# Two transformer blocks in one kernel: depthwise-convolution sums kept in a PSUM bank as two column halves, activation sums split once and reloaded, angle tables moved up, a fifth query unit before the first turn

## The reference, cut to what matters

```python
h = rmsnorm(x) * (1 + scale) + shift          # scale, shift, gate = c @ w_ada + b_ada
glu_a, glu_b, z_conv, q, k, v, z_att, g_conv, g_att = split(h @ w_in)
u = glu_a * sigmoid(glu_b)
u = depthwise_conv(u, conv_w, 31 taps, causal) + conv_b
y_conv = (silu(layernorm(u)) * silu(z_conv)) @ w_conv_out
q, k = partial_rope(q), partial_rope(k)       # cos and sin of position * frequency
# three groups of 8 heads: causal windows with dilation 1, 4, 16; softmax over <= 256 keys
y_att = (merge(three groups) * silu(z_att)) @ w_att_out
x = x + gate * ((sigmoid(g_conv) * y_conv + sigmoid(g_att) * y_att) @ w_o)
```

## Time and the profile before

| | |
|---|---|
| median of 3 runs | 2749.54 us (2749.19 to 2750.30) |
| the profiled execution's own time | 2753.2 us |
| its span | 2751.4 us, granted clock 0.958 |
| PE busy | 2522.0 us (92%), 11800 matmuls |
| DVE busy | 1732.1 us (63%) |
| ACT, POOL busy | 924.9 us (34%), 911.3 us (33%) |
| transfers | 339.09 MB, mean 123 GB/s |

### The profile page before, as it was taken

The page is one execution under the profiler, slowest core; times in us unless marked ns, Lnnn a source line. Parts: engine busy times, 40 slices in busy tenths (PEclk is TensorE's granted clock), DMA queues, the critical chain, the costliest instruction groups (busy, mean ns, idle before and its releaser), DMA issues.

```text
span 2751.4 us, 31479 instructions
## 1 busy us (share of the span) xinstructions
PE 2522.0 (92%) x11800; PEld 2050.0 (75%) x11800; DVE 1732.1 (63%) x2561; ACT 924.9 (34%) x1745; POOL 911.3 (33%) x797
## 2 busy tenths in 40 slices
PE   7899999976779977789999999999999999999997
PEld 4687767954657955557788887887888778787886
DVE  7613668977678878855744653122438686858789
ACT  4114431132321133235500413233116635545453
POOL 3436653525544435642342423222421000000000
PEclk9999989988889988889999999999999999999998
DMA  7413231122332133254433402222527757685754
GB/s 281 129 50 134 96 122 36 62 89 81 102 127 65 55 117 108 94 184 149 146 107 123 150 25 87 74 70 75 182 96 227 201 152 200 153 213 115 208 133 112
DMA packets 180939, 339.09 MB, mean 123 GB/s; under 512 B 21682, under 2 KB 60850, under 8 KB 174260
## 3 DMA queue, kind: packets, MB, share of 16 engines
q1 hardware_dynamic: 160868, 288.33, 31.6%
q0 software_dynamic: 18768, 44.57, 9.0%
q10 hardware_dynamic: 1152, 4.19, 0.4%
HBM read 265.53 MB, written 63.12 MB: 119 GB/s over the span
## 4 chain that ended last, share of the span: by engine, by line
PE 64%; DVE 20%; ACT 5%; issue 4%; DMA 4%; POOL 3%; SPq 1%; DVEq 0%; ACTq 0%; POOLq 0%
PE ps L2737 35%; PE ps L2994 19%; DVE scr L2032 11%; PE ps L2884 4%; POOL w_lo L1323 2%; PE ps L2861 2%; ACT scr L1535 2%; PE ps L2766 1%; PE ps L2847 1%; DMA raw<-in_w_in 1%; ACT w_hi L1575 1%; PE ps L2837 1%; POOL w_hi L1321 1%; DVE w_lo L2096 1%; DVE w_lo L2473 1%
## 5 line engine op out<-in xcount | busy, mean ns | idle before, releaser
L2032 DVE SCALAR_TENSOR_TENSOR scr<-scr,small 128x512 f32<-128x512 f32 x480 | 496.9, 1035 | 15.6
L1321 POOL CAST w_hi<-raw 128x512 fp32r<-128x512 f32 x216 | 157.1, 727 | 801.9 <-DMA raw<-in_w_in 436.7
L2737 PE MATMUL ps<-w_hi,act_hi 128*128 128x512 f32 (+1 forms) x960 | 382.4, 398 | 14.1 <-POOL w_lo L1323 12.6
L2737 PE MATMUL ps<-w_hi,act_lo 128*128 128x512 f32 (+1 forms) x960 | 373.6, 389 | 0.0
L2737 PE MATMUL ps<-w_lo,act_hi 128*128 128x512 f32 (+1 forms) x960 | 373.0, 389 | 0.0
L2994 PE MATMUL ps<-w_hi 128*128 128x512 f32 x896 | 350.6, 391 | 11.0 <-issue 7.5
L2994 PE MATMUL ps<-w_lo,w_hi 128*128 128x512 f32 x896 | 349.4, 390 | 0.0
L2994 PE MATMUL ps<-w_hi,w_lo 128*128 128x512 f32 x896 | 349.2, 390 | 0.0
L2737 PE MATMUL ps<-act_hi,w_hi 128*128 128x512 f32 x768 | 306.8, 399 | 18.0 <-POOL w_lo L1323 6.8
L2737 PE MATMUL ps<-act_lo,w_hi 128*128 128x512 f32 x768 | 305.5, 398 | 0.0
L1323 POOL TENSOR_TENSOR w_lo<-raw,w_hi 128x512 fp32r<-128x512 f32 x216 | 299.2, 1385 | 17.3
(11 more groups left out here) (280 smaller groups left out, 4266.6 us busy)
## 6 DMA issues: line engine op xcount, KB each, us to landing
raw<-in_w_in SPq DMA_DIRECT2D x136, 256.0 KB, 3.2
w_lo<-form_d SPq DMA_DIRECT2D x21, 1024.0 KB, 5.6
late_hi<-h2c_d SPq DMA_DIRECT2D x21, 1024.0 KB, 7.6
raw_c<-in_w_in SPq DMA_DIRECT2D x27, 512.0 KB, 4.7
vreg<-in_w_ada SPq DMA_DIRECT2D x36, 256.0 KB, 5.4
raw<-in_w_in SPq DMA_DIRECT2D x18, 512.0 KB, 4.8
raw<-in_w_up POOLq DMA_DIRECT2D x8, 1024.0 KB, 11.6
late_lo<-in_w_up SPq DMA_DIRECT2D x8, 1024.0 KB, 5.5
```

The costliest lines, as they stand in the source:

```text
L1321: pool.tensor_copy(dhi, src).then_inc(w_hi_done, 1)
L2032: nc.vector.scalar_tensor_tensor(ca, u_in[:, j:j + HALF], w[:, j:j + 1], ca, ALU.mult, ALU.add).then_inc(tap, 1)
L2737: ins = nc.tensor.matmul(out_, lhs, rhs, start=(m == 0), stop=(m == 3 * nk - 1))
```

## The change

1. **Taps.** The running sum of a piece lives in PSUM bank 6 (`ps_c`), and every tap is two instructions on 256 columns. Half e of a tap waits for half e of the tap before, the last but one instruction. The last tap writes `ca` in SBUF, and it alone waits for the store of the piece before. The plan is now 2 a step from step 28 on in g = 0, then 4 a unit, 2 a step, 4 a unit, 2 a step. In a round, DVE's order is: masks and maxima, two steps' taps, evictions, one step's taps, evictions, one step's taps.
2. **Forms.** Only the first four reloads of g = 0 are split by ACT and DVE. Their two parts are stored to DRAM (`parts_d`), and so are the two parts of a21, straight from the projection stage. The other 23 reloads bring both parts, 1 MB each, with nothing for ACT or DVE to do. The store of the plain a21, and DVE's wait for it, go.
3. **Angle tables.** DVE computes the angles ahead of its first block of x, and the two argument reductions behind the second and fourth block; they lie in `ev_more`. SP issues the load of the positions ahead of the adaptive weights.
4. **Order in projection stage 0.** q4 comes before the turn of q0; qt1 and qt2 follow q5 and q6 and so on, and k0 comes before qt6. The loop that runs units together still has four.
5. Waits for the stores of the forms are split by form.

```diff
@@ plan
-                if (t, g) == ("q", 0) and B < LEAD:
+                if (t, g) == ("q", 0) or (t, g, B) == ("k", 0, 0):
                     late.append((t + "t", g, B))
-                    if B == LEAD - 1:
-                        us.append(late.pop(0))
+                    n = {("q", 4): 1, ("q", 5): 2, ("q", 6): 2, ("q", 7): 1, ("k", 0): 1}.get((t, B), 0)
+                    us += late[:n]
+                    late = late[n:]
@@ tap_plan
-    give([("step", 0, s) for s in range(26, 64)], 1)
-    give([(t, 1, B) for t in "qkv" for B in range(NB)], 5)
+    give([("step", 0, s) for s in range(28, 64)], 2)
+    give([(t, 1, B) for t in "qkv" for B in range(NB)], 4)
@@ build
+        ps_c = ps[6][:, :]
-        angs, angc, turns = (scr[:, i * 256:(i + 1) * 256] for i in range(3))
+        angs, angc, turns = (ev_more[:, i // 2, 256 * (i % 2):256 * (i % 2) + 256] for i in range(3))
@@ form_load (SP)
+                if fresh(g, i):
+                    sp.dma_start(form_part(place, 1).bitcast(F32),
+                                 form_d[FORM_DRAM[name]].rearrange("p (k n) -> p k n", k=4)).then_inc(form_ld[place], 16)
+                    return
+                for part in range(2):
+                    sp.dma_start(form_part(place, part).bitcast(F32),
+                                 parts_d[FORM_DRAM[name], part].rearrange("p (k n) -> p k n", k=4)
+                                 ).then_inc(form_ld[place], 16)
+            def parts_store(name, place):
+                for part in range(2):
+                    sp.dma_start(parts_d[FORM_DRAM[name], part].rearrange("p (k n) -> p k n", k=4),
+                                 form_part(place, part).bitcast(F32)).then_inc(parts_st[name], 16)
@@ block_io (SP)
+                if g == 0 and i in (3, 5, 7, 9):
+                    sp.wait_ge(form_lo, (i - 1) // 2)
+                    name = FORM_SEQ[(i - 3) // 2]
+                    parts_store(name, FORM_PLACE[name])
@@ qkv_io (SP)
+                    if u == ("k", 0, 7):
+                        sp.wait_ge(lo_done, SPLIT_LO[("h", 3)])
+                        parts_store("a21", A_SLOT)
@@ DVE, start
+            angles()
             for B in range(NB):
                 x_scale(B)
+                if B in (1, 3):
+                    angle_turns(*((0.0, angs), (0.25, angc))[B // 2])
...
-            dve.wait_ge(a21_st, A21_ST0 + 16)
@@ conv_taps (DVE)
+                    if j == TAPS - 1 and m:
+                        dve.wait_ge(c_st, 16 * m)
+                    for e in range(2):
+                        here, there = slice(256 * e, 256 * e + 256), slice(j + 256 * e, j + 256 * e + 256)
+                        if t:
+                            dve.wait_ge(tap, 2 * t + e - 1)
+                        if j == 0:
+                            nc.vector.tensor_scalar(ps_c[:, here], u_in[:, there], w[:, 0:1],
+                                                    c_cb[:, m // 2:m // 2 + 1], ALU.mult, ALU.add).then_inc(tap, 1)
+                        else:
+                            dst = ca if j == TAPS - 1 else ps_c
+                            nc.vector.scalar_tensor_tensor(dst[:, here], u_in[:, there], w[:, j:j + 1],
+                                                           ps_c[:, here], ALU.mult, ALU.add).then_inc(tap, 1)
@@ block_act_unit (ACT), block_unit_out (DVE)
-                if i in FORM_AT:
+                if i in FORM_AT and fresh(g, FORM_AT.index(i)):
@@ attention (DVE)
-                    for i in units_in(g, b, d):
+                    conv_taps(("step", g, 4 * r))
+                    conv_taps(("step", g, 4 * r + 1))
+                    for i in units_in(g, b, c):
                         block_unit_out(g, i)
-                    for n in range(4):
-                        conv_taps(("step", g, 4 * r + n))
+                    conv_taps(("step", g, 4 * r + 2))
+                    for i in units_in(g, c, d):
+                        block_unit_out(g, i)
+                    conv_taps(("step", g, 4 * r + 3))
```

More of the change, by code:

```diff
@@ L598, in form_part, with fresh, wait_form_load, wait_form @@
             return (w_hi, w_lo)[part][:, 0, k0:k0 + 4, :]
+        def fresh(g, i):
+            return g == 0 and i < FRESH
         def form_loads(g, i):
-            place = FORM_PLACE[FORM_SEQ[i]]
-            per = sum(1 for x in FORM_SEQ if FORM_PLACE[x] == place)
-            return g * per + sum(1 for x in FORM_SEQ[:i + 1] if FORM_PLACE[x] == place)
+            place, n = FORM_PLACE[FORM_SEQ[i]], 0
+            for g_ in range(g + 1):
+                for i_ in range(FORMS if g_ < g else i + 1):
+                    if FORM_PLACE[FORM_SEQ[i_]] == place:
+                        n += 1 if fresh(g_, i_) else 2
+            return n
+        def wait_form_load(eng, g, i):
+            place = FORM_PLACE[FORM_SEQ[i]]
+            eng.wait_ge(form_ld[place], FORM_LD0[place] + 16 * form_loads(g, i))
+        def wait_form(eng, g, i):
+            if fresh(g, i):
+                eng.wait_ge(form_lo, i + 1)
+            else:
+                wait_form_load(eng, g, i)
+        def wait_form_stored(eng, name):
+            eng.wait_ge(form_st[name], FORM_ST0[name] + 16)
+        def wait_parts_stored(eng, name):
+            eng.wait_ge(parts_st[name], PARTS_ST0[name] + 32)
         def block_act(p, part):
@@ L828, in form_load @@
                 place = FORM_PLACE[name]
-                if g == 0 and i == 0:
-                    sp.wait_ge(a21_st, A21_ST0 + 16)
-                    sp.wait_ge(form_st, FORM_ST0 + 16 * 4)
+                if fresh(g, i):
+                    wait_form_stored(sp, name)
+                if g == 0 and i >= 2:
+                    old = {2: "a21", 3: "s2", 4: "s4", 5: "s1", 8: "s3"}.get(i)
+                    if old:
+                        wait_parts_stored(sp, old)
                 if i < 3:
@@ L839, in form_load @@
                     wait_block(sp, 3 * g + 2, 7, 1)
-                sp.dma_start(form_part(place, 1).bitcast(F32),
-                             form_d[FORM_DRAM[name]].rearrange("p (k n) -> p k n", k=4)).then_inc(form_ld[place], 16)
+                if fresh(g, i):
+                    sp.dma_start(form_part(place, 1).bitcast(F32),
[9 more added lines that the diff above has]
+                                 form_part(place, part).bitcast(F32)).then_inc(parts_st[name], 16)
             def block_store(n, p, t):
@@ L935, in conv_load @@
                 if m >= 2:
-                    sp.wait_ge(tap, TAPS * (m - 1))
+                    sp.wait_ge(tap, 2 * TAPS * (m - 1))
                 for hh in range(h + 1):
@@ L946, in conv_store @@
                 t, h = m // 2, m % 2
-                sp.wait_ge(tap, TAPS * (m + 1))
+                sp.wait_ge(tap, 2 * TAPS * (m + 1))
                 sp.dma_start(feature_tile(c_d, t, h), ca).then_inc(c_st, 16)
@@ L1380, in _ @@
                     wait_block(pool, c - 2, 4, 1)
+                if c == 3 and s == 0:
+                    wait_parts_stored(pool, "s1")
                 split_piece(n, raw[:, n % RAW, :], w_hi[:, buffer_of(c), s, :], w_lo[:, buffer_of(c), s, :])
@@ L1488, in qkv_unit @@
                 elif name in ("qt", "kt"):
-                    if g == 0 and name == "qt" and B == 0:
-                        act.wait_ge(a21_st, A21_ST0 + 16)
-                        act.wait_ge(form_st, FORM_ST0 + 16 * 4)
+                    if g == 0 and B == 0:
+                        for form in (("s2", "s3") if name == "qt" else ("s1", "s4")):
+                            wait_form_stored(act, form)
                     if g >= 1 and g < NG and name == "qt" and B == 0:
@@ L2721, in proj @@
                 if m == 0 and (u == ("zc", 0, 1) or name == "q" and t in (1, 2) and h == 4):
-                    pe.wait_ge(form_lo, FORMS * (NG if name == "zc" else t))
+                    wait_form(pe, (NG if name == "zc" else t) - 1, FORMS - 1)
                 s = buffer_of(c)
```

90 lines of the change are left out of this document (43 added, 47 removed).

## The result

The kernel after takes 2548.3 us in the median of 4 runs (2547.66 to 2549.17), against 2749.36 for the kernel before on the same chip (2743.85 to 2750.30): a ratio of 0.9273, 95% interval [0.9257, 0.9289]. That is faster by 201 us. The forecast was 2597 with a range of 2572 to 2650, so it had the sign and the mechanism and missed the size by 49 us, outside its range on the low side. The profiled span is 2545.9 us (2751.4 before).

What follows compares the result with a forecast made beforehand. It took DVE's in-order work, making PE wait in attention 1 and 2, as the bound. Terms +0.5 - 10 - 3 - 6 - 2 - 79.6 - 67.4 + 15 = -152.5 gave 2597 us, range 2572 to 2650.

Steps and rivals of the forecast that it cites:

- What bounds the kernel: Attention 1 and 2: PE waits for exponentials behind overloaded, in-order DVE; some 180 us lie there; PE becomes the bound again.
- the same excess: Attention 1 and 2: each would keep attention 0's 16.5 us over its floor, giving -79.6 and -67.4 us.
- Lateness: Attention 1 and 2: the last two steps' taps stand before the next maxima, 0.5 us a round, 30 rounds, +15.
- The tap: DVE's taps: two halves started 0.335 us apart, 0.67 us a tap, against 1.035 in the mean before.
- Forms: Reloads of forms: 23 more 1 MB loads cost zero; two parts land within 11.2 us, the tightest place allows 14.2.
- Attention 0, projections: Attention 0 gains 3 us of its 16.5 over the floor; projections 1 and 2 gain 6 and 2 us.
- Projection 0: Start and projection 0: the 8.2 us rotation wait goes, -10 us; moved DVE work at the start costs +0.5.
- the first three: Rivals: halves don't overlap, 2633 us (0.10); supply becomes the bound, 2637 us (0.24); DVE's PSUM writes dear, 2895 us (0.05).
- The first: Rival for DVE's taps: halves don't overlap, a tap costs 0.91 us, +36, 2633 us; chance 0.10.
- floors reached to 8 us each and no lateness: Lower bound for attention 1 and 2: stages within 8 us of their floors, no lateness, -32 us more.
- main case: Whole kernel: the forecast's own case, 2575 to 2620 us, chance 0.55, with 0.05 below it.

Runs made afterwards that it cites:

- e5: The kernel after with DVE's old order in a round (masks and maxima, evictions, then all eight taps): 2567.5 us, ratio 0.9338.
- e3: The kernel before with only the taps changed to halves summed in PSUM; old plan, order, forms and start: 2650.3 us, ratio 0.9640.
- e4: The kernel after with the old taps, tap plan and order in a round, so the kernel before plus new forms and start: 2657.2 us, ratio 0.9666.
- e1: The kernel after with each tap one instruction on 512 columns, sum still in PSUM: 2546.5 us, ratio 0.9264.
- e11: The kernel after with each of the 46 reloads of a form's part doubled by a DRAM-to-DRAM copy of the same megabyte: 2613.6 us, ratio 0.9506.
- e12: The kernel before with taps in PSUM halves and the new order of DVE's work in a round; old forms and start: 2584.7 us, ratio 0.9398.
- e7: The kernel after with four pieces of the projection's weights issued on SP ahead of the last ten pieces of adaptive weights: 2539.8 us, ratio 0.9237.
- e8: The kernel after with a third instruction a tap, a multiplication by 1 on the first half, making a tap 1.25 us: 2624.2 us, ratio 0.9542.

## Why the prediction was right in kind and wrong in size

**What bounds the kernel.** Right. The exponentials' waits are gone, PE is the bound of the rounds again, and attention 1 and 2 gave 170 of the 205 us.

**The step that failed: attention 1 and 2.** "I give the others the same excess", 16.5 us each, and on top "still in one order ... 0.5 us a round, 30 rounds, +15". Both were too dear, by 37.8 of the 53 us that the sum is off.

- *Lateness.* With the old order e5 measures 16.2 us in the two stages, but the nearness to my 15 is partly luck: maxima behind taps are the cause, as the term had it, yet 10.1 us fall in two rounds at transitions and not 0.5 in each of thirty. The change has the new order, for which I took nothing off. The term took the last two steps' taps as standing before the next maxima; with DVE's round at about 8.5 us (8 x 0.784 + 2.2) that costs PE nothing that shows: the profile has no wait of PE for exponentials in either stage. The order is the part I undervalued most: 19 us with the other parts in place, 66 with the taps alone.
- *Excess.* It was 8.1 and 2.1 us, not 16.5 each, and in attention 0 itself it is 9.2 now. In attention 1 a single round of 15.6 us, with the wait of 4.2 shown above, makes 4.6 of the 8.1. Attention 0's excess was partly the forms' own. Its longest round, at the first transition between blocks, took 19.9 us; it takes 19.6 with the taps alone (e3), 14.4 with forms and start (e4) and 14.7 after. The text said that the forms' relief is part of the excess, and then subtracted from it a figure that still held forms.

**The tap.** The forecast's 0.67 is 0.784: starts 0.39 apart, not 0.335. The row that I took it from was a copy and a mask. That cost nothing that shows: e1 pays another 0.08 and is no slower. What was right is that the long price goes. A half is 0.48 us long and the next starts after 0.39. So the rule that the prediction cites from the Trainium skill (VectorE: DVE Perf Modes, section The DRAIN you can't avoid), by which it worked out 0.84 and more, doesn't hold here as cited. The prediction left out that the same section excepts a next instruction that isn't held, which starts earlier; the measured 0.39 fits that. And the halves themselves, on which I spent the argument, don't change the time (e1).

**Forms.** Costing the loads at zero held, but "it fits" hid that the fit has an end: with a copy of each megabyte on top it is gone (e11). My estimate of 11.2 us for a pair was safe: in the median the second part lands 8.1 us after its issue.

**Attention 0, projections.** -7.3 for -3; forms and start alone give -8.2 (e4). Projections 1 and 2 gave 11.3 and 9.9 for 6 and 2. Taps alone give 8.3 and 3.4 there, forms and start 1.2 and 3.2, taps with the order (e12) 16.4 and 7.7. So the order helps there too; which instructions make the difference wasn't taken apart.

**Projection 0.** -2.9 for -9.5, the one step that erred to the hopeful side. The wait of 8.2 us did go. But "the k weights then hardly keep up", costed at 1.2 us, was four waits of 3.4 us in all for POOL's split weights and a stretch at half clock (0.50 from 106 to 110 us): 25 matmuls in 12 us where e7 has 58. e7 gets 8 us by removing it.

**Rivals.** None of the first three came. The first had a tap at 0.91 and 2633 us; a tap at 1.25 gives 2624 (e8), so it was also too dear for what it said. The range went wrong at its lower end: the text counted 32 us below its forecast as possible ("floors reached to 8 us each and no lateness") and gave what lay below its main case 5 in 100. That is about what happened in the attention stages, and the projections gave 13 us more than forecast on top.

## What to carry to other kernels

When an in-order engine is overloaded, look at what stands behind each of its waits before making its instructions cheaper: the same taps moved ahead of evictions and subtractions that wait for others were worth 66 us. Remedies for one overload overlap (the order brings 66 us on top of the taps alone, and 19 on top of taps, forms and start), so price each beside the others, and don't carry an excess over from a stage that still holds the cost being removed. When a wait goes, follow the queue of the transfers to see what is late next: four loads issued earlier gave 8 us, and 5 us of work moved ahead of a sum that the same queue waits for took most of it back.

## What the runs showed of the hardware

- No tap with the sum in PSUM (read and written there) was slowed beside POOL: 742 to 760 ns for 512 columns, 472 to 508 for 256. With both inputs in SBUF a half ranges from 465 to 2641, and beside a busy POOL half as many start in the same time.
- A chain of dependent instructions on 512 columns in PSUM starts every 0.86 us for 0.75 us of length; two interleaved halves start every 0.39 us for 0.48.
- POOL's 128x512 subtraction took 1542 to 1554 ns in the mean beside whole taps in SBUF, 1342 beside halves in SBUF and 1303 beside halves in PSUM.
- The same multiplication on 128x256 took 0.43 us in PSUM (0.42 to 0.43) and in the median 0.29 us in SBUF, but there once or more up to 1.92 (e8).
- Doubling the reloads with copies from DRAM to DRAM took a 1 MB part's landing from 5.3 to 11.0 and from 8.1 to 13.3 us.
